# A 31-tap causal convolution split between TensorE and VectorE: 24 taps and 7 taps

## What is computed

```python
def causal_depthwise_conv(u, w, b):          # w: (31, 1024)
    width, ch = w.shape
    out = lax.conv_general_dilated(
        u, w[:, None, :].astype(u.dtype), window_strides=(1,), padding=[(width - 1, 0)],
        dimension_numbers=('NWC', 'WIO', 'NWC'), feature_group_count=ch)
    return out + b

def conformer_conv_module(h, pw1_w, pw1_b, dw_w, dw_b, ln_g, ln_b, pw2_w, pw2_b):
    u = h @ pw1_w + pw1_b
    a, gt = jnp.split(u, 2, axis=-1)
    u = a * jax.nn.sigmoid(gt)
    u = causal_depthwise_conv(u, dw_w, dw_b)
    u = layernorm(u, ln_g, ln_b)
    u = jax.nn.silu(u)
    return u @ pw2_w + pw2_b
```

## Time and profile before

| | us |
|---|---|
| three runs | 1195.27, 1191.06, 1194.42 |
| median | 1194.42 |
| the profiled execution, its own time | 1195.64 |
| its span in the trace | 1193.8 |
| ScalarE's queue issues DMAs until | 12.5 |
| first `pw1` matmul | 33.56 |
| the convolution's mean and variance product starts | 122.35 |
| first expert matmul (L1224) starts | 195.27 |

### The profile page before, as it was taken

The page is one execution under the profiler, slowest core; times in us unless marked ns, Lnnn a source line. Parts: engine busy times, 40 slices in busy tenths (PEclk is TensorE's granted clock), DMA queues, the critical chain, the costliest instruction groups (busy, mean ns, idle before and its releaser), DMA issues.

```text
span 1193.8 us, 20936 instructions
## 1 busy us (share of the span) xinstructions
PE 1012.6 (85%) x7648; PEld 474.6 (40%) x7649; DVE 333.2 (28%) x879; ACT 165.5 (14%) x364; POOL 7.1 (1%) x19
## 2 busy tenths in 40 slices
PE   5999997897999797999887999887999887878774
PEld 3776573433444333444323444323344423232321
DVE  3444456322132222132222122222122221212113
ACT  2334342111011101011101011100011110001001
POOL 1000000000000000000000000000000000000000
PEclk8999997998999998999998989999999999989887
DMA  9983972999999999999999999999999999999991
GB/s 357 280 326 127 389 313 80 420 422 422 422 388 424 422 422 422 422 401 420 423 422 422 422 403 421 422 422 422 422 400 415 422 422 422 422 422 422 422 421 60
DMA packets 84812, 457.39 MB, mean 383 GB/s; under 512 B 9496, under 2 KB 30096, under 8 KB 30992
## 3 DMA queue, kind: packets, MB, share of 16 engines
q1 hardware_dynamic: 83184, 456.29, 94.2%
q10 hardware_dynamic: 1600, 0.71, 0.2%
HBM read 455.93 MB, written 1.05 MB: 383 GB/s over the span
## 4 chain that ended last, share of the span: by engine, by line
PE 59%; DMA 28%; DVE 4%; issue 3%; SPq 2%; ACT 2%; ACTq 1%; DVEq 0%
DMA ring<-in_exp_w 28%; PE bank L1224 25%; PE bank L1247 14%; PE bank L1096 5%; PE bank L1203 3%; PE bank L1080 2%; PE bank L1117 2%; SPq L291 2%; PE bank L1047 2%; PE bank L1191 2%; PE bank L1201 1%; PE bank L1215 1%; PE bank L1234 1%; DVE scratch L877 1%; PE bank L1029 1%
## 5 line engine op out<-in xcount | busy, mean ns | idle before, releaser
L1224 PE MATMUL bank<-ring,xg 128*32 128x256 f32 (+2 forms) x3136 | 449.4, 483 | 60.9 <-DMA ring<-in_exp_w 60.6
L1224 PEld LDWEIGHTS bank<-ring,xg 128*32 128x32 f32 (+2 forms) x3136 | 168.7, 129 | 327.5 <-issue 185.1
L1247 PE MATMUL bank<-ring,actT 128*32 128x512 f32 (+2 forms) x1056 | 220.2, 614 | 21.1 <-DMA ring<-in_exp_w 13.1
L525 ACT ACTIVATE act<-scratch 128x128 f32<-128x128 f32 (+2 forms) x66 | 25.8, 391 | 785.1 <-DVE scratch L877 783.8
L1247 PEld LDWEIGHTS bank<-ring,actT 128*32 128x32 f32 (+2 forms) x1056 | 76.9, 134 | 142.2 <-issue 114.4
L877 DVE TENSOR_SCALAR scratch<-bank 128x128 f32<-128x128 f32 (+2 forms) x66 | 25.6, 387 | 315.1 <-PE bank L1224 315.1
L866 DVE SCALAR_TENSOR_TENSOR acc<-bank,gate,acc 128x512 f32<-128x512 f32 x136 | 93.1, 743 | 58.1 <-PE bank L1203 48.9
L896 DVE TENSOR_TENSOR ysb<-bank,g2half 128x512 f32<-128x512 f32 x29 | 20.1, 692 | 221.5 <-PE bank L1247 221.5
L1191 PEld LDWEIGHTS bank<-onehot_bf,arena 128*128 128x128 bf16 x1584 | 56.8, 102 | 23.0 <-issue 23.0
L1203 PE MATMUL bank<-ysb,onehotT 64*128 64x512 f32 x240 | 62.4, 628 | 3.0 <-DVE ysb L896 2.1
L1191 PE MATMUL bank<-onehot_bf,arena 128*128 128x32 bf16 (+2 forms) x1584 | 60.3, 196 | 1.0 <-DVE arena L796 1.0
(11 more groups left out here) (214 smaller groups left out, 496.2 us busy)
## 6 DMA issues: line engine op xcount, KB each, us to landing
ring<-in_exp_w SPq DMA_DIRECT2D x396, 1024.0 KB, 24.2
ring<-in_ada_w SPq DMA_DIRECT2D x24, 1024.0 KB, 10.3
ring<-in_conf_pw_w SPq DMA_DIRECT2D x12, 1024.0 KB, 11.7
acc<-in_x SPq DMA_DIRECT2D x1, 1024.0 KB, 4.9
out<-acc SPq DMA_DIRECT2D x2, 512.0 KB, 2.7
g2full<-in_ada_b SPq DMA_DIRECT2D x1, 512.0 KB, 4.6
xT<-in_final_norm_g ACTq DMA_DIRECT2D x1, 512.0 KB, 3.4
b1f<-in_exp_b SPq DMA_DIRECT2D x1, 256.0 KB, 4.2
```

The source lines that it names most:

```text
L525: a.activation(act[:, h * c:(h + 1) * c], g_lim[h][:, 0:c], ACT.Sigmoid, scale=ALPHA).then_inc(sig_ready, 1)
L1224: ins = mm(up_to(m, n, r), xg[:, b, k, 0:m], wk[:, at:at + span(m)], start=False, stop=(k == KT - 1))
L1247: ins = mm(dst, actT[:, f % (2 * q), at:at + m], wk[:, f % 2 * D + r * H:f % 2 * D + (r + 1) * H], start=(f < sides), stop=(f >= KT - sides))
```

## The change

Six tap steps (taps 0 to 23, the 24 oldest inputs) stay with TensorE. The seven others (taps 24 to 30, inputs 6 to 0 tokens back) go to VectorE, one multiply-add of a whole 128 x 256 tile each, read from the gated tile itself. For that `ubuf` gets eight columns in front that GpSimd sets to zero, and moves to another place. The sums run in two halves (even and odd m), are joined, and the bias is in one of them. VectorE then adds TensorE's part from PSUM (`all_taps`); ScalarE only squares, from `conv`. The shifted copies become 246 to 249 tokens long. The tap weights come with 12 DMAs as before and one for the seven late rows; TensorE turns those with eight more transposes into `dwcol`.

```diff
+        LATE = TAPS - PE_STEPS * SHIFTS
+        SEEN = PE_STEPS * SHIFTS - SHIFTS + T
+        UB = 8
...
+        dwlate = xgflat[0:LATE, 2 * P:2 * P + D]
+        ubuf = xgflat[:, 2 * P + D:2 * P + D + 2 * (UB + T)].rearrange("p (b s) -> p b s", b=2)
+        late = act[:, 0:2 * T].rearrange("p (b s) -> p b s", b=2)
+        dwcol = sb("dwcol", [P, KT, LATE])
...
+            pool.memset(ubuf, 0.0).then_inc(s_pad, 1)
             pool.memset(ushift, 0.0).then_inc(s_pad, 1)
...
-            for q in range(STEPS):
-                there = min(SHIFTS, TAPS - SHIFTS * q)
+            for q in range(PE_STEPS):
                 for h in range(2):
-                    a.dma_start(dwrow[16 * q:16 * q + 16, h, 0:there, :],
-                                dw_w[0, SHIFTS * q:SHIFTS * q + there, h * 512:(h + 1) * 512].rearrange(
+                    a.dma_start(dwrow[16 * q:16 * q + 16, h, :, :],
+                                dw_w[0, SHIFTS * q:SHIFTS * q + SHIFTS, h * 512:(h + 1) * 512].rearrange(
                                     "j (g c) -> g j c", c=BLK)).then_inc(s_dw, 16)
+            a.dma_start(dwlate, dw_w[0, PE_STEPS * SHIFTS:TAPS, :]).then_inc(s_dw, 16)
...
-            def conv_out(t):
-
-                a.wait_ge(p_taps, t + 1)
-                a.activation(conv[:, t, :], bank[3 + t % 2][:, 0:T], ACT.Identity,
-                             bias=vcol[:, DB + t:DB + t + 1]).then_inc(s_conv, 1)
+            def conv_squared(t):
+
+                a.wait_ge(s_conv, t + 1)
                 if t >= 2:
                     a.wait_ge(s_stat, t - 1)
-                a.activation(csq[:, t % 2, :], bank[3 + t % 2][:, 0:T], ACT.Square,
-                             bias=vcol[:, DB + t:DB + t + 1]).then_inc(s_csq, 1)
+                a.activation(csq[:, t % 2, :], conv[:, t, :], ACT.Square).then_inc(s_csq, 1)
...
+            v.tensor_copy(dwcol[:, :, :], bank[5][:, 2 * P:2 * P + KT * LATE].rearrange("p (k m) -> p k m", k=KT)
+                          ).then_inc(v_dw, 1)
...
-                v.tensor_tensor(taps_w[:, t % 2, :, :, :],
+                v.tensor_tensor(taps_w[:, t % 2, 0:PE_STEPS, :, :],
...
+            def late_taps(t):
+
+                last = [0, 0]
+                for m in range(LATE):
+                    side = m % 2
+                    w = dwcol[:, t, m:m + 1]
+                    at = UB + PE_STEPS * SHIFTS + m - PAD
+                    seen = ubuf[:, t % 2, at:at + T]
+                    if m < 2:
+                        first = v.tensor_scalar(late[:, side, :], seen, w, vcol[:, DB + t:DB + t + 1] if side else 0.0,
+                                                ALU.mult, ALU.add)
+                        last[side] = step(first)
+                    else:
+                        v.wait_ge(dve, last[side])
+                        last[side] = step(v.scalar_tensor_tensor(out=late[:, side, :], in0=seen, scalar=w,
+                                                                 in1=late[:, side, :], op0=ALU.mult, op1=ALU.add))
+                v.wait_ge(dve, n[0])
+                link(v.tensor_tensor(conv[:, t, :], late[:, 0, :], late[:, 1, :], ALU.add))
+
+            def all_taps(t):
+
+                v.wait_ge(p_taps, t + 1)
+                v.tensor_tensor(conv[:, t, :], conv[:, t, :], bank[3 + t % 2][:, 0:T], ALU.add).then_inc(s_conv, 1)
...
                 if t + 1 < KT:
                     tap_weights(t + 1)
                 if t:
+                    all_taps(t - 1)
+                late_taps(t)
+                if t:
                     sums(t - 1)
+            all_taps(KT - 1)
             sums(KT - 1)
...
+            for k in range(KT):
+                ins = tr(bank[5][:, 2 * P + k * LATE:2 * P + (k + 1) * LATE], dwlate[:, k * P:(k + 1) * P],
+                         ident[0:LATE, 0:LATE])
             ins.then_inc(p_dw, 1)
...
                 if t >= 2:
-                    pe.wait_ge(s_csq, t - 1)
-                for q in range(STEPS):
+                    pe.wait_ge(s_conv, t - 1)
+                for q in range(PE_STEPS):
```

More of the change, by code:

```diff
@@ L25 @@
 SHIFTS = 4
+PE_STEPS = 6
 BLK = 32
@@ L445, in _ @@
                 if t:
-                    conv_out(t - 1)
+                    conv_squared(t - 1)
             a.activation(fin[:, 0:1], eps[:, :], ACT.Sqrt)
-            conv_out(KT - 1)
+            conv_squared(KT - 1)
             a.wait_ge(p_st, 2)
@@ L646, in _ @@
                           ).then_inc(v_dw, 1)
-            v.wait_ge(v_dw, 1)
+            v.tensor_copy(dwcol[:, :, :], bank[5][:, 2 * P:2 * P + KT * LATE].rearrange("p (k m) -> p k m", k=KT)
+                          ).then_inc(v_dw, 1)
+            v.wait_ge(v_dw, 2)
             v.wait_ge(s_eye, 1)
@@ L654, in tap_weights @@
                 at = NB * (t % 4)
-                v.tensor_tensor(taps_w[:, t % 2, :, :, :],
-                                wcol[:, t // 4, :, at:at + NB].unsqueeze(3).to_broadcast([P, STEPS, NB, BLK]),
-                                eye[:, :].unsqueeze(1).unsqueeze(1).to_broadcast([P, STEPS, NB, BLK]),
+                v.tensor_tensor(taps_w[:, t % 2, 0:PE_STEPS, :, :],
+                                wcol[:, t // 4, 0:PE_STEPS, at:at + NB].unsqueeze(3).to_broadcast([P, PE_STEPS, NB, BLK]),
+                                eye[:, :].unsqueeze(1).unsqueeze(1).to_broadcast([P, PE_STEPS, NB, BLK]),
                                 ALU.mult).then_inc(s_tapw, 1)
@@ L663, in gated @@
                     v.wait_ge(s_sa, t - 1)
-                v.scalar_tensor_tensor(out=ubuf[:, t % 2, :], in0=bank[1 + t % 2][:, 0:T],
+                v.scalar_tensor_tensor(out=ubuf[:, t % 2, UB:UB + T], in0=bank[1 + t % 2][:, 0:T],
                                        scalar=vcol[:, PB1 + t:PB1 + t + 1], in1=glu[:, t % 2, :],
@@ L688, in sums @@
                     v.tensor_tensor(stat[:, T:2 * T], stat[:, T:2 * T], csq[:, t % 2, :], ALU.add).then_inc(s_stat, 1)
-            v.wait_ge(s_pad, 2)
+            v.wait_ge(s_pad, 3)
             tap_weights(0)
@@ L1065, in _ @@
             turn_row(0)
-            pe.wait_ge(s_dw, 16 * 2 * STEPS)
+            pe.wait_ge(s_dw, 16 * (2 * PE_STEPS + 1))
             for h in range(2):
-                ins = tr(bank[5][:, h * P:(h + 1) * P], dwrow[:, h, :, :].rearrange("p j c -> p (j c)"), ident[:, :])
+                tr(bank[5][:, h * P:(h + 1) * P], dwrow[:, h, :, :].rearrange("p j c -> p (j c)"), ident[:, :])
+            for k in range(KT):
+                ins = tr(bank[5][:, 2 * P + k * LATE:2 * P + (k + 1) * LATE], dwlate[:, k * P:(k + 1) * P],
+                         ident[0:LATE, 0:LATE])
             ins.then_inc(p_dw, 1)
@@ L1081, in taps @@
                                  ushift[:, t % 2, g, SHIFTS * q:SHIFTS * q + T],
-                                 start=(q == 0), stop=(q == STEPS - 1))
+                                 start=(q == 0), stop=(q == PE_STEPS - 1))
                 ins.then_inc(p_taps, 1)
```

11 lines of the change are left out of this document (5 added, 6 removed).

## The result

The changed kernel takes 1185.71 us (median of six runs, 1183.57 to 1186.42), the kernel before in the same sessions 1194.08 us (1191.06 to 1195.27): a ratio of 0.9932, 95% interval 0.9918 to 0.9946. That is 8.4 us less, with an interval of 6.4 to 9.8. The forecast was 1187, in a range of 1184 to 1192.

What follows compares the result with a forecast made beforehand. TensorE was taken to bound the convolution loop and weights the expert loop, whose start sets the end. Start 1.5, transposes 0.0, taps 5.4 and stage end 0.7 made 7.6 us: 1188.0 or 1186.8, given as 1187, range 1184.0 to 1192.0.

Steps and rivals of the forecast that it cites:

- What bounds the kernel: TensorE bounds the convolution loop at 10.69 us a turn; a shift in reaching the experts moves the end equally.
- Start: ScalarE's queue before the loop: 16 DMA issues become 13 at 0.504 us each, 1.5 us sooner (1.0 to 2.0).
- rival A: Start gives less through issue cost, late clock or transposes: 0.7 to 1.2 us lost, 1187.5 to 1188.5; A or B or both 0.26.
- also covered: At the start, the first pw1 chunk is nearly there by 30 us, before it is wanted at 32.1.
- Eight transposes: TensorE's added transposes before the first pw1 fit a 0.89 us gap and cost nothing (bound 0 to 0.4).
- TensorE's taps: In the convolution loop a tap piece falls from 3.59 to 2.69 us, six times 0.90: 5.4 us.
- VectorE's turn: VectorE's work per loop turn is 8.5 us (8.2 to 9.4), under TensorE's 9.79, with late taps 3.05.
- Rival B: VectorE runs serially, late taps 3.9 us, turn 9.4, stage end gains nothing: 1187.6; A or B or both 0.26.
- End of the stage: From the last pw1 to the product of the means VectorE is the bound; 0.7 us gained of a possible 1.7.
- X: The end of the last pw1 in the convolution stage, 111.78 before; the product then followed 10.57 later.
- Sum: Whole kernel: 1.5 + 0.0 + 5.4 + 0.7 = 7.6 us gained, giving 1187.
- Rival C: VectorE bounds the loop from a turn of 9.2 to 9.4, gain gone at 10.2; short of all 0.04, slower 0.05.

Runs made afterwards that it cites:

- the two delays: Changed kernel with eight or sixteen useless 128 x 128 copies on ScalarE ahead of vcol at the start; 1186.39 and 1188.82 us.
- second profile of the changed kernel: The changed kernel run once more, nothing edited; 1184.74 us (0.9920 of the kernel before).
- the run of one chain: Changed kernel with its late taps as one chain, each multiply waiting for the one in front, no joining add; 1185.85 us (0.9927).
- the one with 13 issues: Kernel before with only the first 13 of its 16 tap-weight DMAs issued, missing weights zero; 1187.47 us (0.9948), a time that can't be used.
- four steps: Changed kernel with four TensorE tap steps for tiles 0 to 6, their copies on ScalarE; second run also reorders start and last tile's copies; 1185.52 and 1184.29 us.
- seven steps: Changed kernel with seven tap steps on TensorE and three late taps on VectorE, run twice; 1184.67 and 1183.83 us.
- five steps: Changed kernel with five tap steps on TensorE and eleven late taps on VectorE; 1188.99 us (0.9954).
- five steps balanced: Changed kernel with five tap steps for tiles 0 to 6, six for the last, copies split by tile between VectorE and ScalarE; 1178.29 us (0.9866).

## Why the prediction was right, point by point

- *What bounds the kernel.* Right. The loop stayed TensorE's, and a shift ahead of the experts arrived at their start unchanged in the two profiles compared (7.10 and 7.11). That it arrives at the end too is borne out by the two delays, to about a microsecond.
- *Start.* Forecast 1.5, measured 1.30 at the first `pw1`. The new issue costs 0.35 us and not 0.504, so ScalarE gained 1.54; TensorE's sixteen matmuls took 6.50 instead of 6.26, so 0.24 of it was lost there, the sign and the order of what rival A allowed. In the second profile of the changed kernel they took 5.90, and the first `pw1` matmul, at 32.16, waited 0.78 us for its chunk instead. So one step was wrong though it cost little: "also covered" for the first `pw1` chunk. I had put bytes moved by 30 us equal to chunks landed. In the six profiles in which TensorE waits for that chunk it is complete only at 31.9 to 32.8. The cover was at most 0.4 us, not 2, and the changed kernel has used up the start.
- *Eight transposes.* Forecast nothing, measured nothing: they end at 31.96, and TensorE then still waits 0.30 us for `hT`.
- *TensorE's taps.* Forecast 2.69 for a piece and 5.4 in all, measured 2.73 and 5.16. The pieces shrink by 0.86, a little less than in proportion.
- *VectorE's turn.* Forecast 8.5, measured 8.58; late taps forecast 3.05, measured 3.11 from the first start to the end of the joining add (100.69 to 103.80). Rival B fell with this row, since the multiplies overlap; the run of one chain shows what serial instructions cost, 3.52 us (100.78 to 104.30) where B had 3.9.
- *End of the stage.* Forecast a product at X + 9.85, measured X + 9.93: 0.64 gained for 0.7.
- *Sum.* Forecast 7.6, measured 7.1 up to the experts by the profiles and 8.4 by the medians, with 7.1 inside the interval. That 1187 lies within 1.3 us of the median owes a little to luck: the sum held nothing for the end of the expert stage, which alone differs by 3.6 us between the two profiles.
- *Rival C.* Did not occur, but the point from which it decides was well placed: at a turn of 9.9 the loop is VectorE's. Its price was too low by 1.2 us at the end of the chain.

**What the sum left out** is the difference of 1.3 us between the two figures, which may be scatter, and what happens behind the last weights. From the first expert matmul to the landing of the last chunk that the chain waits for it is 941.3 us in the kernel before and 941.6 in the changed one; the 3.6 us arise behind it. The chain there, of the kernel before:

```profile
1142.20 4.55 issue
...
1147.81 16.32 PE bank L1224 x54
...
1168.10 9.68 PE bank L1247 x32
```

and of the changed kernel:

```profile
1133.93 5.93 issue
...
1140.92 15.82 PE bank L1262 x64
...
1160.31 7.11 PE bank L1285 x32
```

Two things are in it. One is TensorE's pace: the same 32 matmuls take 9.68 us at a granted clock of 0.73 or 7.11 at 1.00, and there are no more weights on their way that would hide it. Over the thirteen profiles they take from 7.11 to 9.69; the changed kernel has 7.11 once and 8.01 once, so this part is not the same in every execution of a kernel.

The other is the row "issue": ahead of the last expert TensorE stands for 4.55 and 5.93 us although it waits for nothing that the profile shows. Nine of the thirteen profiles have this stall, of 4.2 to 5.9 us: the kernel before, the one with 13 issues, the changed kernel twice, the one chain, both delays and both runs with four steps. The four others, seven steps twice, five steps and five steps balanced, haven't. Seven steps, first profile:

```profile
1124.76 29.19 DMA ring<-in_exp_w
1153.98 1.96 PE bank L1262 x8
...
1159.71 8.08 PE bank L1285 x32
```

There TensorE goes on at once and waits for the chunks of the last expert as they land. It is done with the last expert's first products 964.5 to 965.2 us after the first expert matmul, in the kernel before, the changed kernel, the one chain and the delays at 968.3 to 968.9. So the stall costs some 3.7 us, and the pace of what follows decides another 2 to 3. With both, the expert stage is 998.5 us before, 994.9 and 996.4 changed, 998.0 one chain, 995.0 and 997.5 the delays; without the stall 992.7 and 992.9 seven steps, 992.6 five steps, 992.1 balanced; with four steps it is 998.6 and 992.5, the last with its weights in 2 us sooner.

The stall goes with TensorE's own program: all five profiles whose TensorE code is that of the changed kernel have it, both of seven steps haven't. Why it is there is not shown; no run was made that moves only the place of that code. It means that more than half of the 6.5 us by which the balanced kernel beats the changed one is not owed to the balance of the convolution.

## What to carry to other kernels

Work can be moved from the engine that bounds a loop to one with idle time as long as the receiver's own turn stays under the new, shorter turn; write both turns out from the starts of instructions in the timeline (here 8.6 against 9.8), and count in the first and the last turn, where the receiver is alone on the path: there 0.64 us came of a possible 1.7. Then look at what stands behind the changed part: here an idle time of TensorE ahead of the last expert came and went with the number of tap steps and was worth some 3.7 us. Two interleaved chains of dependent instructions, each waiting for the one two places in front, cost 0.40 us a step on VectorE where one chain costs 0.52. And before a start is made shorter, look for the landing of the chunk that the first big product needs; bytes moved don't tell it.

## What was not expected of the hardware

- From 12 to 23 us the kernel before shows a granted clock of 0.50 to 0.69, the changed kernel 1.00, and the sixteen matmuls between took 6.26 us in the one and 6.50 in the other. The changed kernel:

```profile
16.00:22.00 6.00, 5.72 (x14) 4.59 (x15) 0.00 (x0) 2.36 (x3) 0.00 (x0) 1.00 1.03 399
```

The same kernel's sixteen matmuls of the same line and shape, later on:

```profile
157.35 3.62 PE L1064 MATMUL bank<-scratch,mean_of 128*128 128x256 f32 x16
```

So a granted clock of 1.00 in a window is no proof that TensorE ran at 2.4 GHz there; the distance of its instructions tells more.

- After a stall of 2.2 us in the run with four steps, a tap piece took 3.62 us instead of 1.93, at a granted clock of 0.54, in a stage where TensorE had never left the full clock. A short wait can cost its own length once more. At the start of the loop it was the same: after waits for chunks the first block of `pw1` took 15.77 us with five steps and 17.04 in the second run with four, instead of 14.05, at a granted clock of 0.50 for part of it.
- A DMA's issue on ScalarE's queue costs 0.32 to 0.34 us for three rows of 4 KB, 0.35 for seven, 0.40 to 0.42 for eleven, 0.47 for fifteen, and 0.50 for 64 pieces of 128 bytes. So most of the price belongs to the issue and not to its size; by these rows I estimate 0.3 us for an issue and 0.01 for each row.
- VectorE's multiply-add with one column operand takes 0.35 us for 128 x 256, with two 0.41 (L694 above).
